# Attention of a hybrid decoder block: the lower keys' rescaling of differential blocks issued on ScalarE instead of GpSimd

## The reference, cut to what matters

```python
for each head h (4), each block of 128 queries:
    s = q @ k.T * scale + alibi_bias          # two score maps n = 0, 1, each [128, 2048]
    s = where(mask, s, -inf)
    p = softmax(s, axis=-1)
    a = p[:, :, 0] - lam * p[:, :, 1]
    o = a @ v                                 # v is 128 wide
    o = rmsnorm(o, g_sub) * (1 - lam_init)
```

## Time and profile before

| | us |
|---|---|
| median of three runs | 3035.59 |
| lowest and highest | 3033.98, 3035.62 |
| the profiled execution's own time | 3035.42 |
| its span in the trace | 3033.3 |

### The profile page before, as it was taken

The page is one execution under the profiler, slowest core; times in us unless marked ns, Lnnn a source line. Parts: engine busy times, 40 slices in busy tenths (PEclk is TensorE's granted clock), DMA queues, the critical chain, the costliest instruction groups (busy, mean ns, idle before and its releaser), DMA issues.

```text
span 3033.3 us, 39287 instructions
## 1 busy us (share of the span) xinstructions
PE 2919.0 (96%) x14082; PEld 2404.6 (79%) x14082; DVE 1664.0 (55%) x2505; ACT 1022.3 (34%) x1975; POOL 975.2 (32%) x720
## 2 busy tenths in 40 slices
PE   7999999998998999988999999999999999999998
PEld 5888888777877777777887888888887788888887
DVE  5211111389899898897556444444446544444445
ACT  4111111287786786875222111111112111111112
POOL 4220020157458365564114122212224222221222
PEclk9999999999999999999999999999999999999999
DMA  5343342733433334142752011011126101111113
GB/s 175 122 150 102 110 137 96 191 80 92 120 89 89 92 99 119 38 116 91 215 171 97 31 55 55 28 55 55 55 77 226 58 28 55 55 45 38 55 41 125
DMA packets 206424, 282.78 MB, mean 93 GB/s; under 512 B 12064, under 2 KB 136224, under 8 KB 206304
## 3 DMA queue, kind: packets, MB, share of 16 engines
q1 hardware_dynamic: 152160, 213.19, 24.3%
q10 hardware_dynamic: 53376, 67.25, 6.2%
q0 software_dynamic: 768, 0.79, 0.1%
HBM read 196.38 MB, written 84.80 MB: 93 GB/s over the span
## 4 chain that ended last, share of the span: by engine, by line
PE 47%; DVE 2%; DMA 1%; POOL 1%; issue 1%; ACT 1%; SPq 0%; DVEq 0%; ACTq 0%; POOLq 0%; PEldq 0%
PE ml_ps_y L2117 7%; PE ml_ps_y L2119 7%; PE ml_ps_y L2121 7%; PE ml_ps_u L2108 7%; PE ml_ps_u L2109 7%; PE ml_ps_u L2110 7%; PE mo_acc L1689 2%; PE mo_acc L1687 2%; PE mo_acc L1688 2%; DMA ml_dn_raw<-in_w_down_dram 1%; DMA out_dram<-ml_xres 1%; PE mo_acc L1675 0%; DVE ml_u_hi L2028 0%; DVE ml_relu L2025 0%; DVE ml_y L2036 0%
## 5 line engine op out<-in xcount | busy, mean ns | idle before, releaser
L2068 DVE TENSOR_TENSOR ml_y<-ml_y,ml_ps_y 128x512 f32<-128x512 f32 x496 | 340.7, 687 | 220.5 <-PE ml_ps_y L2121 215.3
L2117 PE MATMUL ml_ps_y<-ml_dn_hi,ml_u_hi 128*128 128x512 f32 x992 | 390.4, 394 | 11.2 <-DVE ml_y L2068 11.2
L2119 PE MATMUL ml_ps_y<-ml_dn_lo,ml_u_hi 128*128 128x512 f32 x992 | 386.8, 390 | 0.0
L2121 PE MATMUL ml_ps_y<-ml_dn_hi,ml_u_lo 128*128 128x512 f32 x992 | 386.6, 390 | 0.0
L2108 PE MATMUL ml_ps_u<-h_rows_hi,ml_up_hi 128*128 128x512 f32 x992 | 385.9, 389 | 0.0
L2109 PE MATMUL ml_ps_u<-h_rows_lo,ml_up_hi 128*128 128x512 f32 x992 | 385.9, 389 | 0.0
L2110 PE MATMUL ml_ps_u<-h_rows_hi,ml_up_lo 128*128 128x512 f32 x992 | 385.9, 389 | 0.0
L1294 DVE TENSOR_REDUCE at_nmax<-at_ps_s 128x1 f32<-128x1024 f32 (+7 forms) x384 | 347.1, 907 | 47.0 <-PE at_ps_s L1398 42.7
L2025 DVE TENSOR_TENSOR ml_relu<-ml_relu 128x512 f32<-128x512 f32 x128 | 94.5, 738 | 472.9 <-ACT ml_relu L1984 472.9
L1886 POOL TENSOR_TENSOR ml_up_lo<-ml_up_raw,ml_up_hi 128x1024 fp32r<-128x1024 f32 x62 | 162.0, 2631 | 492.7 <-ACT ml_up_hi L1956 492.7
L1893 POOL TENSOR_TENSOR ml_dn_lo<-ml_dn_raw,ml_dn_hi 128x1024 fp32r<-128x1024 f32 x62 | 148.3, 2414 | 497.2 <-ACT ml_dn_hi L1974 497.2
(11 more groups left out here) (247 smaller groups left out, 5765.3 us busy)
## 6 DMA issues: line engine op xcount, KB each, us to landing
qk<-pj_out_sb ACTq DMA_DIRECT2D x64, 512.0 KB, 2.8
ml_dn_raw<-in_w_down_dram SPq DMA_DIRECT2D x32, 1024.0 KB, 7.6
ml_up_raw<-in_w_up_dram SPq DMA_DIRECT2D x31, 1024.0 KB, 5.7
at_q<-qk SPq DMA_DIRECT2D x96, 256.0 KB
at_k<-qk SPq DMA_DIRECT2D x96, 256.0 KB
vals<-pj_out_sb ACTq DMA_DIRECT2D x32, 512.0 KB, 2.9
at_v_sb<-vals SPq DMA_DIRECT2D x32, 512.0 KB, 3.9
pj_raw<-in_w_in_dram SPq DMA_DIRECT2D x24, 512.0 KB, 4.0
```

The source lines that it names most:

```text
L2068: dve.tensor_tensor(y[:, t, cols], y[:, t, cols], ps_y[:, b % 4, :], ALU.add)\
L2117: pe.matmul(ps_y[:, b % 4, :], u_hi[:, s, f, rows], hi[:, f, cols], start=(start and f == 0), stop=False)
L2119: pe.matmul(ps_y[:, b % 4, :], u_hi[:, s, f, rows], lo[:, f, cols], start=False, stop=False)
L2121: last = pe.matmul(ps_y[:, b % 4, :], u_lo[:, s, f, rows], hi[:, f, cols], start=False, stop=(stop and f == FT - 1))
```

## The change

For differential blocks the step `fix` goes to ScalarE: an activation that copies 128 x 1024 fp32 in place with `corr` as its per-partition scale. It has a semaphore of its own, `rescaled`, on which both kinds of mix wait. FoX blocks keep `fix` on GpSimd. The planner's table gives the moved step the engine ACT and 1.1 in place of 2.0, and all steps around it are put in order anew. The diff, cut to its core:

```diff
@@ attention_steps
             if sc.part and (fox or sc.s == 0):
-                walk.step("fix", (b.n, sc.a), "POOL", 2.0, at + RUSH["fix"], [("corr", sc), ("exp", parts[0])])
+                walk.step("fix", (b.n, sc.a), *(("POOL", 2.0) if fox else ("ACT", 1.1)), at + RUSH["fix"],
+                          [("corr", sc), ("exp", parts[0])])
@@ GpSimd
-                if what == "fix":
+                if what == "fix" and blocks[arg[0]].kind == FOX:
...
-                        pool.wait_ge(fixed, fix_no[arg])
+                        pool.wait_ge(rescaled, fix_no[arg])
@@ ScalarE
+                elif what == "fix" and blocks[arg[0]].kind == DIFF:
+                    n, a = arg
+                    low = probs[:, places[n, a]:places[n, a] + 1024]
+                    first, second = (sc for sc in scores if (sc.b, sc.a) == arg and side(sc) == 0)
+                    act.wait_ge(corrected, top_no[second.g] + 1)
+                    act.wait_ge(exped, first.g + 1)
+                    act.activation(low, low, ACT.Copy, scale=corr[:, n % SETS, a, 0:1]).then_inc(rescaled, 1)
@@ VectorE
-                        dve.wait_ge(fixed, fix_no[arg])
+                        dve.wait_ge(rescaled, fix_no[arg])
```

More of the change, by code:

```diff
@@ L1007, in attend @@
     top_no = {sc.g: n for n, sc in enumerate(sc for sc in scores if sc.part == 1)}
-    fix_no = {at: n + 1 for n, at in enumerate((sc.b, sc.a) for sc in scores
-                                              if sc.part == 1 and (blocks[sc.b].kind == FOX or sc.s == 0))}
+    fix_no = {at: n + 1 for kind in (FOX, DIFF) for n, at in enumerate(
+        (sc.b, sc.a) for sc in scores if sc.part == 1 and blocks[sc.b].kind == kind and (kind == FOX or sc.s == 0))}
     tile_no, chain_done, mix_done = {}, {}, {}
@@ L1066, in attend @@
         fixed = r.sem("fixed")
+        rescaled = r.sem("rescaled")
         chained = r.sem("chained")
```

## The result

The changed kernel takes 3053.97 us (median of six, 3050.25 to 3056.24), the kernel before beside it 3035.42 (six, 3033.98 to 3036.00): 1.0061 of the time, interval 1.0048 to 1.0074, so **18.5 us slower**. Forecast were 3019 us and a gain of 16.5. The profiled execution took 3054.11, its span is 3051.6 against 3033.3.

A forecast was written before the change was run, and what follows sets the result against it. PE bounds the kernel (96% busy), DVE the J = 3 stretches. Per head 4.1 (mix) + 2.2 (clock) - 2.2 (ScalarE) = 4.1 us, 16.5 over four heads, from 3035.4 to a forecast of 3019 us; range 3004 to 3034.

The forecast's parts named there:

- What bounds the kernel, and where its loss was: PE 96% busy overall; in four J = 3 stretches DVE bounds and PE loses some 9 us each.
- DVE's mix, 3.7 + 0.4 us per head: J = 3 stretch: mixes of blocks 9 and 8 no longer meet GpSimd's work, gaining 4.1 us per head.
- GpSimd's backlog gone, with a margin of about 2 us when DVE's mix runs: Block 9: without fixes GpSimd's last mix ends at 729.7, before DVE's mix, which had started at 731.82.
- The clock, 2.2 us per head: Behind PE's gap in J = 3 stretches: gap shrinks to 1 to 2 us, so lost clock time returns.
- ScalarE, 1.5 + 0.7 us per head: Loss from 32 added activations: 1.5 us in the J = 3 stretch, 0.7 in the next, 2.2 per head.
- 6.3: Gain per head in us, from DVE's mix and the clock, before ScalarE's loss is taken off.
- The new semaphore costs nothing: Both mixes wait for `rescaled`, but the chain they need comes later, so nothing queues behind this wait.
- The replanned order: Scores issued earlier in the new order might gain; the forecast gave nothing for that.
- The test that the forecast named: A head's second stretch should not grow; over 1 us would mean the J = 2 block's activations are not hidden.
- B: Rival: ScalarE replaces DVE as bound, exponentials late by every `fix`; 2.1 us per head slower, 3044 us; chance 0.08.

The follow-up runs named there:

- e3: Kernel before with its order kept and the differential blocks' rescaling left out on every engine: 3021.21 us, 0.9948 of the kernel before.
- e1: Kernel before with its order kept on every engine, the differential blocks' rescaling issued by ScalarE instead of GpSimd: 3023.16 us, 0.9959 of the kernel before.
- e7: Rescaling on ScalarE, order of before except the new order in the FoX blocks behind heads, in three pieces: 3031.61 us, 0.9985 of the kernel before.
- e4: Changed kernel's order, with the differential blocks' rescaling left out on every engine: 3055.64 us, 1.0062 of the kernel before.
- e2: Changed kernel's order on every engine, but the rescaling run by GpSimd: 3067.56 us, 1.0111 of the kernel before.
- e12: Order of before, only the J = 3 blocks rescaled on ScalarE, the J = 2 blocks on GpSimd: 3028.46 us, 0.9978 of the kernel before.
- e11: Rescaling on ScalarE, new order only in blocks 10 and 11, block 10's a = 0 mix moved ahead of block 11's first chain: 3039.02 us, 1.0011 of before.

## Why the prediction was wrong, point by point

- **What bounds the kernel, and where its loss was**: right. With nobody rescaling and the order kept (e3) the long gap is gone.
- **DVE's mix, 3.7 + 0.4 us per head**: right. Free instructions take 0.88 and 1.28, against an assumed 0.87 and 1.27; block 8's takes 0.87. (0.87 less 0.1 is 0.77 and not 0.79, as the working has it; the pace measured is 0.79, 733.61 - 732.82.) With the order of before, PE's gap shrinks by 3.5 us (5.36 to 1.84), nearly all of the 3.7.
- **GpSimd's backlog gone, with a margin of about 2 us when DVE's mix runs**: right for block 9, where the margin is 4.2 us (GpSimd's last addition ends at 728.65, the mix starts at 732.82). Not looked at was block 10's mix, which in the new order meets GpSimd's mix of block 11 (1.14 for 0.34 us).
- **The clock, 2.2 us per head**: over-sized. With the order of before, PE's gap is the forecast 1.84 us in every head, but the clock falls behind it all the same in two heads of e1 and in all four of e3, so 1.4 and 0.6 us per head came back. That a gap of this size costs no clock did not hold. In the changed kernel the clock is 1.00 in the J = 3 stretch of three heads, and falls 30 us later in three of the four, at a place where the forecast had none to lose.
- **ScalarE, 1.5 + 0.7 us per head**: over-sized as a whole. The medians of e1 and e3 differ by 0.5 per head; by blocks and with the clock set aside it is an estimated 0.3 in the J = 3 stretch, thought dear, and 0.86 in the J = 2 block, near the 0.7. The gain without any `fix` is 14.3 us (e3), 3.6 per head, where 6.3 stood; most of what is missing is the clock. With the order of before the change itself gains 12.4 us (e1) against the 16.5 forecast: two terms too large, in opposite directions, so part of that nearness is luck.
- **The new semaphore costs nothing**: right; no wait in the changed kernel's views is put down to it.
- **The replanned order**: this is the step that failed. The text on the change said that the orders differ in blocks 9 to 13 (and the same places of the other heads) and nowhere else, and the sum gave nothing for the new order: "scores are issued earlier in the new order" was taken as a possible gain only, and a cost of the order itself was not thought of. Both are wrong. The step lists differ from the turns of block 7 to the scores of block 17; e7's part of that, among the FoX blocks behind each head, costs 8.4 us. The new order as a whole costs 31 to 34 us, twice what the engine move was to gain. What it brought is PE waits of 1.9 to 2.2 us where there were none, and behind some of them the low clock. It costs that with no ScalarE instruction added at all (e4), so none of the rivals held either: B, the rival on this side, wanted ScalarE as the bound and 3044 us. That "more DVE steps stand before it" was written down as cover for GpSimd, where it should have been read as lateness of what PE waits for.
- **The test that the forecast named** pointed at the right place with the wrong reason: "the second stretch of a head should not grow; if it does by more than 1 us, the activations of the J = 2 block are not hidden". It grew by 2.7 us in block 9 and up to 5.3 in block 10. But e4, with the new order and no activation at all, has the same 2.7 in block 9, so in the new order the activations account for none of it that shows.

## What to carry to other kernels

Where one table both assigns work to engines and sets the order of everything, a change of one entry is two changes. Price them apart: keep the old order and change only the issuing engine (e1), and the other way round (e2). Here the move alone was worth 12 us and the reorder that came with it cost 31. And count what a new gap does to the clock behind it: of what block 10 lost in the changed kernel, most was time at the low clock. The stretch in which the bounding engine was 97% busy was not safe ground here but the most exposed one: read the new order there for every wait of that engine, and ask how much queued work still stands ahead of each.

## What the runs showed of the hardware beyond that

- A small instruction pays for meeting another engine as a large one does, and GpSimd pays too: in e12 its 128 x 4 multiplication took 1.18 us behind DVE's mix, and 0.20 in the changed kernel, where nothing was in its way.
- ScalarE's copy with a per-partition scale, SBUF to SBUF in place, 128 x 1024 fp32, took 1135 to 1156 ns in all 32 cases. None was stretched, though GpSimd's mixes ran beside some of them (1.15 us at 706.75, beside a GpSimd multiplication from 706.07 to 707.97), whereas GpSimd's `fix` of the same shape ranged from 1882 to 2471 ns.
- PE's granted clock fell to 0.50 behind gaps that were all small (the longest 1.07 us, 3.7 in sum within ten, e11), as it had behind a single one of 5.4. Whether it falls, and for how long, differed between heads with the same gaps: in the changed kernel 0.57 over 12 us, 0.57 over 8, no fall, and 0.57 over 12. With e1's gap of 1.84 us it fell in two heads of four, with e3's in all four. That scatter sets how exactly a single head's loss can be known.
